# RWKV blocks: decay matrices behind the last sum, two compressions in eight pieces, the next block's transposes ahead of the chunks

## The reference, cut to what matters

```
def step(S, xs):
    rt, wt, kt, vt, kkt, at = xs
    S = (S * jnp.exp(wt)[:, :, None, :]
         - jnp.einsum('bhvk,bhk->bhv', S, kkt)[..., None] * (kkt * at)[:, :, None, :]
         + vt[..., None] * kt[:, :, None, :])
    return S, jnp.einsum('bhvk,bhk->bhv', S, rt)
```

## Time and profile before

| what | us |
|---|---|
| median of 3 runs | 1535.96 |
| lowest and highest of them | 1530.56, 1542.29 |
| span of the profiled execution, first to last instruction | 1521.9 |
| TensorE busy in it | 1390.8 (91%) |
| VectorE busy in it | 810.5 (53%) |
| mean granted TensorE clock | 0.924 |

### The profile page before, as it was taken

The page is one execution under the profiler, slowest core; times in us unless marked ns, Lnnn a source line. Parts: engine busy times, 40 slices in busy tenths (PEclk is TensorE's granted clock), DMA queues, the critical chain, the costliest instruction groups (busy, mean ns, idle before and its releaser), DMA issues.

```text
span 1521.9 us, 27930 instructions
## 1 busy us (share of the span) xinstructions
PE 1390.8 (91%) x9786; PEld 990.9 (65%) x9786; DVE 810.5 (53%) x2042; ACT 406.2 (27%) x787; POOL 168.6 (11%) x312
## 2 busy tenths in 40 slices
PE   5998989998899999898999899998889999988895
PEld 2673777887875576464558467778888746755542
DVE  1355566756544845862116365575665467477610
ACT  4230101312111145651431211031111221646400
POOL 0000000000000064520000000000000002645000
PEclk9997899999779999999999879998986899999998
DMA  7231342331004155784242324224100141665701
GB/s 321 71 113 56 111 138 60 92 104 57 1 1 155 56 158 172 224 300 155 79 172 57 111 64 176 64 63 140 56 2 1 32 178 56 185 212 149 299 1 69
DMA packets 92928, 171.73 MB, mean 113 GB/s; under 512 B 14081, under 2 KB 79794, under 8 KB 86898
## 3 DMA queue, kind: packets, MB, share of 16 engines
q1 hardware_dynamic: 79778, 120.39, 23.9%
q0 software_dynamic: 13008, 49.54, 9.5%
HBM read 157.08 MB, written 21.12 MB: 117 GB/s over the span
## 4 chain that ended last, share of the span: by engine, by line
PE 71%; DVE 15%; issue 8%; ACT 3%; DMA 1%; SPq 0%; POOL 0%; DVEq 0%; POOLq 0%; ACTq 0%
PE bank L581 16%; PE bank L618 12%; PE bank L1188 8%; PE bank L2801 4%; PE bank L514 2%; PE bank L1214 2%; PE bank L814 2%; PE bank L1322 2%; PE bank L1310 1%; DVE area L1680 1%; DVE area L1715 1%; PE bank L822 1%; PE bank L800 1%; PE bank L584 1%; PE bank L1299 1%
## 5 line engine op out<-in xcount | busy, mean ns | idle before, releaser
L581 PE MATMUL bank<-stream,hT 128*128 128x512 f32 (+3 forms) x768 | 261.6, 497 | 0.5 <-DVE hT L451 0.5
L618 PE MATMUL bank<-hT,stream 128*128 128x272 f32 x960 | 225.8, 396 | 5.6 <-DVE area L1558 5.4
L618 PEld LDWEIGHTS bank<-hT,stream 128*128 128x128 f32 x960 | 182.3, 191 | 44.4 <-DVE area L1558 6.0
L581 PEld LDWEIGHTS bank<-stream,hT 128*128 128x128 f32 x768 | 145.9, 194 | 100.2 <-issue 86.5
L1188 PE MATMUL bank<-stream,prm 128*128 128x256 f32 x512 | 126.3, 409 | 0.4 <-DVE YT L1539 0.4
L2801 PE MATMUL bank<-stream,YT 128*128 128x512 f32 x256 | 114.3, 609 | 4.8 <-DVE YT L2709 4.8
L1188 PEld LDWEIGHTS bank<-stream,prm 128*128 128x128 f32 x512 | 104.8, 207 | 18.0 <-issue 1.4
L2801 PEld LDWEIGHTS bank<-stream,YT 128*128 128x128 f32 x256 | 49.5, 195 | 67.2 <-issue 61.9
L407 POOL DMA_DIRECT2D stream<-in_slcK x128 | 69.0, 549 | 169.2 <-PE bank L584 135.5
L407 POOL DMA_DIRECT2D stream<-in_slcV x128 | 68.5, 539 | 72.3 <-PE bank L2253 30.0
L2817 DVE TENSOR_TENSOR X<-bank,X 128x512 f32<-128x512 f32 x16 | 11.1, 692 | 102.4 <-PE bank L2801 102.4
(11 more groups left out here) (634 smaller groups left out, 2286.6 us busy)
## 6 DMA issues: line engine op xcount, KB each, us to landing
stream<-in_cmpL SPq DMA_DIRECT2D x256, 128.0 KB, 2.3
stream<-in_win_ SPq DMA_DIRECT2D x12, 2048.0 KB, 7.6
stream<-in_slcK SPq DMA_DIRECT2D x128, 64.0 KB, 2.3
stream<-in_slcK POOLq DMA_DIRECT2D x128, 64.0 KB, 2.5
stream<-in_slcV SPq DMA_DIRECT2D x128, 64.0 KB, 2.8
stream<-in_slcV POOLq DMA_DIRECT2D x128, 64.0 KB, 2.8
stream<-in_wout SPq DMA_DIRECT2D x4, 2048.0 KB, 11.0
out_winpast<-in_winraw POOLq DMA_DIRECT2D x2, 4064.0 KB, 26.6
```

Source lines behind the costliest of these rows:

```text
L581: last = nc.tensor.matmul(ps[:, 0:w], hT[:, k, tok(i)], ws[:, k, :], start=(k == 0), stop=(k == KT - 1))
L618: last = nc.tensor.matmul(ps[:, 0:HALF], ws[:, k, 128 * f:128 * f + 128], hT[:, k, HALF * s:HALF * s + HALF], start=(k == 0), stop=(k == K ...
```

## The change

Four edits, all in phase R:

1. The turns (t1, t2) leave `pe_r_products` and become `pe_r_turn`. Block 0's stands where it was; block m + 1's stands between block m's `pe_r_solve` and `pe_r_chunks`, so ahead of the wait for the fifth sum.
2. Compressions 6 and 7 are cut. A part is four matmuls of 128x256. Block m computes half a compression (its keys or its values: block 0 keys of 6, block 1 values of 6, block 2 keys of 7, block 3 values of 7) into a bank of its own, four matmuls at level 3 and four at level 4, each ahead of the wait for the sum.
3. VectorE takes that half (a copy and an addition of 256 columns in place of 512) behind the fifth sum.
4. The four MTc matrices are built behind the fifth sum and that half, in place of behind the third.

```
             pe_compress(pe, l, 5)
+            pe_r_turn(pe, l, 0)
             for m in range(4):
                 pe_r_products(pe, l, m)
                 pe_r_solve(pe, l, m)
+                if m < 3:
+                    pe_r_turn(pe, l, m + 1)
                 pe_r_chunks(pe, l, m)
...
+        def spread(m):
+            return 6 + m // 2, m % 2
+
+        def pe_compress_part(pe, l, b, c, part):
+
+            w1p = Q("w1p").rearrange("p (c j e) -> p c j e", c=2, j=8)
+            cs = slot("cmp", l, b).rearrange("p (g j c m) -> p g j c m", g=NPAGE, j=8, c=2)
+            if part == 0:
+                pe.wait_ge(sem_of_slot("cmp", l, b), at("here", "cmp", l, b))
+                pe.open("abc", l, b, c)
+            ps = bank("abc", l, b, c)
+            for j in range(4 * part, 4 * part + 4):
+                last = nc.tensor.matmul(ps[:, 0:256], w1p[:, c, j, :], cs[:, :, j, c, :], start=(j == 0), stop=(j == 7))
+            if part:
+                pe.full(last.then_inc(pe_done, 1), "abc", l, b, c)
+                if c:
+                    pe.name("used", "cmp", l, b)
+
+        def dve_compress_part(dve, l, b, c):
+
+            dve.wait_ge(pe_done, at("full", "abc", l, b, c))
+            ps = bank("abc", l, b, c)
+            lo, hi = slice(0, 64), slice(64, 128)
+            t = TMP[:, 256 * c:256 * c + 256]
+            if b % 2 == 0:
+                dve(nc.vector.tensor_copy(t[lo], ps[hi, 0:256]).then_inc(dve_done, 1))
+                dve(nc.vector.tensor_tensor(HIDD[lo, b // 2, c, 0:254], ps[lo, 0:254], t[lo, 2:256], ALU.add).then_inc(dve_done, 1), "HID", l, b)
+            else:
...
+            dve.free("abc", l, b, c)
...
-        def pe_r_products(pe, l, m):
+        def pe_r_turn(pe, l, m):
...
                 pe.full(last.then_inc(pe_done, 1), key, l, m)
+
+        def pe_r_products(pe, l, m):
+
             ps = pe.open("bn", l, m)
...
-                if lev == 3 and m < 2:
-                    pe_compress(pe, l, 6 + m)
+                if lev >= 3:
+                    pe_compress_part(pe, l, *spread(m), lev - 3)
                 pe.wait_ge(dve_done, at("Z", l, m, lev))
...
                 elif lev == 2:
+                    dve_r_ahead(dve, l, m + 1, 3)
+                elif lev == 3:
+                    dve_r_ahead(dve, l, m + 1, 4)
+                else:
+                    dve_compress_part(dve, l, *spread(m))
                     for c in range(4):
                         dve(nc.vector.tensor_tensor(MTc[:, c], bc(C("IDN2"), 1, 2), E3[m % 2][:, :, 32 * c + 31:32 * c + 32].broadcast_to([128, 2, 64]),
                                                   ALU.mult).then_inc(dve_done, 1))
-                    dve_r_ahead(dve, l, m + 1, 3)
-                elif lev == 3:
-                    if m < 2:
-                        dve_compress(dve, l, 6 + m)
-                    dve_r_ahead(dve, l, m + 1, 4)
```

More of the change, by code:

```diff
@@ L1190, in pe_compress @@
             pe.name("used", "cmp", l, b)
+        def spread(m):
[22 more added lines that the diff above has]
+            else:
+                dve(nc.vector.tensor_copy(t[hi], ps[lo, 0:256]).then_inc(dve_done, 1))
+                dve(nc.vector.tensor_tensor(HIDD[hi, b // 2, c, 0:254], ps[hi, 2:256], t[hi, 0:254], ALU.add).then_inc(dve_done, 1), "HID", l, b)
+            dve.free("abc", l, b, c)
         def dve_compress(dve, l, b):
```

## The result

The changed kernel's median is 1492.11 us (four runs, 1487.33 to 1499.05) against 1539.12 for the kernel before in the same comparison (1530.56 to 1543.34): recorded ratio 0.975, interval 0.9707 to 0.9793. The quotient of the two medians is 0.969, just under that interval. So it is faster, by 2.5% by the ratio and 3.1% by the medians; the forecast was 1507.5, its range 1488 to 1524.

What follows compares the result with a forecast made beforehand. TensorE, busy 91% of the span, loses time waiting for VectorE or at its lower clock, both in phase R. Terms -21.5 - 9.3 - 1.1 + 3.0 + 0.5 = -28.4 us: span 1493.5, plus 14.1 gives 1507.5, range 1488 to 1524.

Steps and rivals of the forecast that it cites:

- The tails: Eight stretches from L1310 of level 3 to L1330, the solve's end: 7.24 us each, 57.9 for 79.4, -21.5 us.
- "rx" to the last chunk, and the border: L1330 to last chunk matmul: 39.2 for 48.5, -9.3 us; six borders up to the first product: 10.8 for 11.9, -1.1.
- the wait forecast for "pN": At the border, pN waits until VectorE copied t2, so the first product starts at 1.8 us, before 1.37 at high clock.
- Products to level 3: Six stretches, products and levels 0 to 2: unchanged work, more clock falls, mean 20.6 for 20.1, +3.0 us.
- Banks and weights: Later banks shift: layer 0 loses a 0.21 wait, layer 1's score unit waits up to 0.69, +0.5 us; weight loads hidden.
- The median of before is 14.1 above that span; taken over: Last step, whole kernel: the 14.1 us between before's median and profiled span added to span 1493.5, giving 1507.5.
- the clock holds: Rival: clock stays up through the border, all products stretches 17.45 and chunks 4.60; -49.7 us, so 1486; chance 0.18.

Runs made afterwards that it cites:

- the second profile of before: The kernel before, unchanged, profiled once more: 1518.77 us, span 1517.1, granted clock 0.928, against 1521.9 and 0.924 in the first profile.
- the run at 1468.37: Changed kernel with the turns put back behind the chunks, edits 2 to 4 standing: 1468.37 us, ratio 0.9536 against the kernel before.
- The kernel with the banks apart: Changed kernel with two banks skipped ahead of "bn" in blocks 1 to 3, so "bn" and "pN" take long-free banks: 1473.95 us, ratio 0.9588.

## Why the prediction was right, and where it was off

**The tails.** Forecast 7.24 each, 57.9 in all; measured 7.25 and 58.03. Every term of the sum held, block 2's too, which got longer as forecast.

**"rx" to the last chunk, and the border.** Forecast 39.2 + 10.8 = 50.0; measured 48.23. The stretch without a border (block 3) takes 4.59, those with one 6.4 at the full clock, so a border is 1.8, as worked out from the two copy chains. The only wait the profile names is that of "bn". At the border shown t2's last copy begins at 315.44, takes 0.42, and the products begin only at 316.17, since "bn" itself took 1.01 there, at the lower clock. At the next border, where the clock is up, t2's last copy runs from 350.88 to 351.30 and the first product starts at 351.36: 0.06 behind it, and 0.70 behind the start of "bn" (350.66) where 0.44 is enough without a wait. That is the wait forecast for "pN", hidden in the row by the end of "bn".

**Products to level 3.** Forecast +3.0, measured +2.8. The place is right: six borders of six let the clock fall in place of three (two in the second profile of before), as the prediction expected more falls there. That the size agrees to 0.2 is luck: against the second profile of before the difference is +6.5 (123.39 for 116.88), and for "rx" to product -14.1 (48.23 for 62.30) in place of -12.2; the tails' is -22.3 in place of -21.4. The reason given was that the chunks and a pause now stand together without full-size work. Its second half holds better than its first: with tails of 7.25 us, each kernel that puts 0.8 us or more of full-size work back has no fall, while taking the pause away alone leaves six falls.

**Banks and weights.** Layer 1's score unit waits 0.44 (0.69 was the bound); layer 0's wait of 0.21 is gone:
```profile
1309.83 0.71 PE L2311 MATMUL bank<-area,X 64*128 64x128 f32 x6 [0.44 <-DVE area L2758]
```
T4's later load made no wait. All told the span fell by 32.7, for a forecast of 28.4.

**The step that was off** is "The median of before is 14.1 above that span; taken over". The profiled execution after took 1490.86 us with a span of 1489.2: only 1.7 lies around a span. It is 1.7 in other runs too (1512.86 and 1511.2, 1547.8 and 1546.1). The 14.1 of before wasn't something around the span; it was that its timed runs had a lower granted clock than its profiled one. The runs of before in all comparisons go from 1512.86 us at a mean clock of 0.929 to 1547.8 at 0.907. A clock 0.022 lower is 4.4% of the time at half speed, 67 us, which costs TensorE half of that, 34; the difference is 35. With 1.7 in place of 14.1 the forecast would have been 1495.2, for 1492.11 measured.

**What the prediction didn't see.** It took the clock of before as given and asked what each edit moves. It didn't ask what edits 2 and 3 would do to the clock with the turns left alone. The answer is the run at 1468.37: the tails win 21.4 in the profile, and 31 more come in the same regions (260.4 to 207.7 is 52.7), because the clock no longer falls in them at all: the seven falls at the tails' waits are gone with the waits, and those at the borders don't come while the turns stand there. The change as made keeps about 9 of these 31 and edit 1 gives up the rest. On the kernel before, edit 1 had less to lose, since the clock fell in most blocks anyway (eleven falls with and without it); so the run with the turns alone, even or 1% faster, does not contradict it. The rival "the clock holds", with 1486, named that gain for the wrong kernel: it is true only with the turns back.

The Trainium skill (TensorE: Matmul & The Clock Gate, section "Part 4: PE-mode transpose") says that transposes don't count as busy for the clock the way other work does. The runs here differ from that, in float32: eight transposes in a border (0.82 us) keep it at 1.00 as four matmuls (0.89 us) do. By that rule moving the turns would have been free for the clock; without the move the kernel is 24 us faster. The Trainium skill (same page, section "A second HAM failure mode: psum-queue depth-cycling") says that short idle moments from going round the PSUM banks make the clock swing. The kernel with the banks apart agrees in part: low time 58 to 27 us. But it has as many falls, and the one at 383.44 in the kernel after comes with no idle moment in the 4.43 us before it; that is not in that rule.

**Left open.** How the clock is decided within a border, and whether the moment at which a border comes has a part in it. Why 0.4 us of full-size work at a border is no better than none once the wait is gone (low time 27 and 30 us against 27, medians 1481.18 and 1478.20 against 1473.95). A single fall lasts from 3.4 to 23.9 us in these traces, so a sum of low time scatters much. With that, with scatter like that of the two profiles of before, and from sets measured apart, I don't rank these three. The low time outside the regions (139 to 149 us in the versions that have none within them) was not worked on.

## What to carry to other kernels

Price each edit against the version without it and not against the kernel before: here one edit of four cost as much as the other three gained in the tails, and the sum hid it. Before moving full-size work off a place where TensorE has only small matmuls and a short wait, look for the granted clock there; what the move can win is the work's own length at most (here 0.44 of 0.93 us a border, and that only with the bank wait gone), and what it can lose is part of the next stretch, here up to 7.7 us (25.12 for 17.45). And when buffers go round in order, moving two opens earlier moves a wait to whatever opens a full round later.

## What the runs showed of the hardware

- Full-size work of 0.8 to 0.9 us between 32-row matmuls and the products, in six places, went with 0 us at the lower clock in two regions of 104 us, against 27 without it (58 where a wait of 1.03 us stood there too), and it made no difference whether it was transposes or matmuls. That holds for tails of 7.25 us without a wait of 0.9 at level 4: with that wait back the clock fell at two borders of six, the turns in place.
- The matmuls of "rx" to the last chunk (128x64 and 32x64 operands) kept TensorE busy without a gap for 4.43 us, and the clock fell while they ran (383.44, after). They don't bring it down each time: with the turns back the same matmuls ran at 1.00 in all eight blocks.
- The spread of the kernel before, 1513 to 1548 us, goes with the granted clock (0.929 to 0.907). The version whose regions stay at the full clock still spreads over 1462.52 to 1472.14, with clocks from 0.953 to 0.958.
- The device time of an execution is its span and 1.7 us, so run times at different mean clocks are what a span must be compared with.
